# Clearing of DRAM rows moved to SyncE's queue, gelu steps moved back, the first expert's begin reordered, and the last block's second rows added by TensorE

## The reference

```python
def forward(x, ...):
    for l in range(2):
        h = rmsnorm(x, norm_mix[l])
        u = h @ w_in[l]                                   # all head groups' inputs
        a = rg_lru(causal_conv(x_lru)) * gelu(y_lru)      # recurrence, gated
        b = mla_group(q_dn, kv_dn, k_pe)                  # 6 heads, causal
        c = nsa_group(q, kc, vc, ks, vs, kw, vw, gates)   # 6 heads, three branches
        x = x + concat(a, b, c) @ w_out[l]
        h = rmsnorm(x, norm_ffn[l])
        if l == 0:
            x = x + (silu(h @ wg) * (h @ wu)) @ wd        # d_ff 2816
        else:
            top_val, top_idx = top_k(h @ router_w, 2)
            w = softmax(top_val)
            for e in range(8):                            # d_ff 1408 each
                x = x + gate[:, e] * ((silu(h @ wg[e]) * (h @ wu[e])) @ wd[e])
    return rmsnorm(x, norm_final)
```

## Time and profile before

| | us |
|---|---|
| median of 3 runs | 1330.28 |
| lowest, highest | 1328.93, 1330.73 |
| the profiled execution, its own time | 1324.21 |
| its span, first to last instruction | 1322.4 |
| TensorE busy in it | 1267.1 (96%) |
| VectorE | 949.1 (72%) |
| ScalarE | 677.8 (51%) |
| GpSimd | 130.1 (10%) |

### The profile page before, as it was taken

How to read it: one execution, slowest core, us unless ns; L and a number is a source line. 1 busy time by engine, 2 the same in 40 slices (tenths; PEclk the granted TensorE clock), 3 DMA queues, 4 the chain that set the end, 5 groups by cost and what they waited for, 6 DMA issues and landing times.

```text
span 1322.4 us, 24758 instructions
## 1 busy us (share of the span) xinstructions
PE 1267.1 (96%) x10314; PEld 819.6 (62%) x10375; DVE 949.1 (72%) x1304; ACT 677.8 (51%) x993; POOL 130.1 (10%) x113
## 2 busy tenths in 40 slices
PE   7999999999999999999999999979999999999992
PEld 3457565444444444444457565569979988989981
DVE  7886885886531556334886885688788799989996
ACT  6256774443210333112265774365586687787772
POOL 0011320600000000031011000501200000000002
PEclk9999899999999999999999999999999999999997
DMA  8551881444310443012551000168999999999975
GB/s 272 184 151 35 317 334 60 146 186 149 118 67 0 150 165 148 0 33 103 194 150 35 20 1 21 61 238 325 360 381 376 349 348 398 374 352 398 359 307 208
DMA packets 43134, 260.26 MB, mean 197 GB/s; under 512 B 6522, under 2 KB 7546, under 8 KB 28554
## 3 DMA queue, kind: packets, MB, share of 16 engines
q1 hardware_dynamic: 33626, 224.77, 46.1%
q0 software_dynamic: 8960, 33.26, 7.0%
q10 hardware_dynamic: 432, 0.59, 0.1%
HBM read 218.00 MB, written 33.65 MB: 190 GB/s over the span
## 4 chain that ended last, share of the span: by engine, by line
PE 84%; issue 6%; DVE 4%; DMA 3%; POOL 1%; ACT 1%; SPq 0%; POOLq 0%; DVEq 0%; ACTq 0%
PE bank L1177 20%; PE bank L1178 20%; PE bank L1179 19%; PE bank L1387 5%; PE bank L1435 3%; PE bank L1405 3%; PE bank L727 1%; PE bank L726 1%; PE bank L725 1%; DMA expert_slots<-arena,row_index 1%; PE bank L735 1%; PE bank L737 1%; PE bank L736 1%; POOL expert_slots L2520 1%; PE bank L1242 1%
## 5 line engine op out<-in xcount | busy, mean ns | idle before, releaser
L988 DVE SCALAR_TENSOR_TENSOR arena<-arena 128x3072 f16<-128x3072 f32 x86 | 288.2, 3352 | 10.8 <-ACT arena L842 9.1
L842 ACT ACTIVATE arena<-arena 128x3072 f16<-128x3072 f32 x86 | 237.9, 2767 | 41.1 <-DMA arena<-in_ew 19.5
L1177 PE MATMUL bank<-arena 128*128 128x144 bf16 (+3 forms) x877 | 215.1, 264 | 6.0 <-DVE arena L988 2.7
L1178 PE MATMUL bank<-arena 128*128 128x144 f16 (+3 forms) x878 | 215.4, 264 | 0.1
L1179 PE MATMUL bank<-arena 128*128 128x144 bf16 (+3 forms) x867 | 211.2, 263 | 0.0
L1178 PE MATMUL bank<-hl,wring_hi 128*128 128x512 f16 x352 | 133.4, 379 | 1.5 <-issue 0.6
L1179 PE MATMUL bank<-hh,wring_lo 128*128 128x512 bf16 x341 | 129.2, 379 | 0.0
L1177 PE MATMUL bank<-hh,arena 128*128 128x512 bf16 x338 | 128.1, 379 | 1.0
L1178 PE MATMUL bank<-hl,arena 128*128 128x512 f16 x338 | 128.1, 379 | 0.0
L1177 PE MATMUL bank<-hh,wring_hi 128*128 128x512 bf16 (+1 forms) x333 | 126.3, 379 | 1.0 <-DVE wring_lo L1885 0.5
L1179 PE MATMUL bank<-hh,arena 128*128 128x512 bf16 x319 | 120.9, 379 | 0.0
(11 more groups left out here) (334 smaller groups left out, 2521.2 us busy)
## 6 DMA issues: line engine op xcount, KB each, us to landing
arena<-in_ew SPq DMA_DIRECT2D x86, 1536.0 KB, 9.1
arena<-in_dw SPq DMA_DIRECT2D x22, 1536.0 KB, 6.4
wstage<-in_w_chunk SPq DMA_DIRECT2D x44, 512.0 KB, 3.9
expert_results<-iota POOLq DMA_DIRECT2D x9, 2048.0 KB
arena<-in_cmp_w SPq DMA_DIRECT2D x2, 2048.0 KB, 8.0
arena<-arena SPq DMA_DIRECT2D x60, 64.0 KB, 2.1
expert_slots<-iota POOLq DMA_DIRECT2D x5, 512.0 KB
expert_results<-wstage SPq DMA_DIRECT2D x5, 512.0 KB
```

The costliest lines, as they stand in the source:

```text
L842: act.activation(ew_hi_[:, G % EP, :], ew[:, G % ES, :], ACT.Copy, scale=SW).then_inc(M["hi_ready"], 1)
L988: dve.scalar_tensor_tensor(out=ew_lo_[:, G % EP, :], in0=ew[:, G % ES, :], scalar=SW, in1=ew_hi_[:, G % EP, :], op0=ALU.mult, op1=ALU.subt ...
L1177: pe.matmul(out, w_hi, x_hi, start=first, stop=False)
L1178: pe.matmul(out, w_hi, x_lo, start=False, stop=False)
```

## The change

It has five parts.

1. The 19 DMAs that clear DRAM rows are issued by SyncE (`clear_rows`) in layer 0, ahead of its load of chunk 18; GpSimd issues none. `blank` counts them alone, and `load_rows` waits for `slotted`.
2. In both layers GpSimd's gelu steps wait for the maximum of score step 3.
3. The first expert's begin: TensorE does all 64 gather products in a row and then `upper(0)` and `upper(1)`; ScalarE turns the third weight part after all eight copies, and runs a silu of one column ahead of the first part, which loads the table.
4. `places` is a generator of four parts, of which VectorE runs one in each of the steps G = 4 to 7; the row numbers come in the third, the flag in the fourth.
5. In the tail block 3 (`SUMMED`) is added by TensorE: identity times the sum with the first rows, then a diagonal matrix of the second gates times the second rows, both in fp32 into two PSUM banks, which ScalarE's square and VectorE's last scaling read. VectorE does block 3's first addition ahead of the others, makes the diagonal, and leaves out its second addition.

```diff
@@ experts_pe
             def begin():
+                pe.wait_ge(M["gathered"], KC // 2)
+                pe.wait_ge(M["first_hi"], 1)
+                upper(0)
                 pe.wait_ge(M["first_hi"], 2)
                 upper(1)
...
                 if j == KC // 2:
-                    pe.wait_ge(M["gathered"], KC // 2)
-                    pe.wait_ge(M["first_hi"], 1)
-                    upper(0)
                     pe.wait_ge(*ready("tok_l", TT - 1))
@@ experts_act
+            act.activation(small[:, 244:245], eps[:, 0:1], ACT.Silu)
             first_hi(0)
             for j in range(KC):
                 gathered(0, j, bank[GATHER_BANK[j % 4]], 0, CAPS[0])
-                if j in (3, 5):
-                    first_hi(j // 2)
-            for p in (3, 4):
+                if j == 3:
+                    first_hi(1)
+            for p in (2, 3, 4):
                 first_hi(p)
@@ experts_dve
-                if G == 2 * LEAD:
-                    places()
+                if G >= 2 * LEAD:
+                    next(place_parts, None)
@@ experts_sp, load_rows
-                sp.wait_ge(*ready("blank", "slotted"))
+                sp.wait_ge(*ready("slotted"))
@@ tensor, behind the experts
+            for i in SUMMED:
+                pe.wait_ge(*ready("first_added", i))
+                for half in range(2):
+                    pe.matmul(banks[:, 2 * i + half, :], ident[:, :], xtok[i][:, half * 4:(half + 1) * 4, :],
+                              start=True, stop=False)
+            for i in SUMMED:
+                pe.wait_ge(*ready("first_added", "diagonal", i))
+                pe.wait_ge(*ready(f"second_row{i}"))
+                for half in range(2):
+                    mm = pe.matmul(banks[:, 2 * i + half, :], diagonal[i - SUMMED[0]],
+                                   second_row[i][:, half * T:(half + 1) * T], start=False, stop=True)
+                mm.then_inc(*signal("second_summed", i))
@@ scalar, tail
-                act.wait_ge(*ready("second_added", i))
-                act.activation(xtok[i], by_chunk(second_row[i]), ACT.Square,
+                act.wait_ge(*(ready("second_summed", i) if i in SUMMED else ready("second_added", i)))
+                act.activation(xtok[i], by_chunk(with_second(i)), ACT.Square,
@@ vector, tail
-            for i in range(TT):
+            for i in (*SUMMED, *range(SUMMED[0])):
...
+            for i in SUMMED:
+                dve.tensor_scalar(diagonal[i - SUMMED[0]], ident[:, :], gate_second[:, i:i + 1], None,
+                                  ALU.mult).then_inc(*signal("first_added", "diagonal", i))
             for i in range(TT + 1):
-                if i < TT:
+                if i < SUMMED[0]:
                     dve.wait_ge(*ready(f"second_row{i}"))
@@ gpsimd, gelu steps, both layers
+                    pool.wait_ge(*ready("nmx", l, 3, 0))
                     pool.wait_ge(*ready("feat", l, feat_index("y", c)))
...
-                if l == 0:
-                    pool.wait_ge(*ready("nmx", l, 0, 0))
-                    blank = results_dram.rearrange("(p a) d -> p (a d)", p=P).rearrange("p (a n) -> p a n", n=256)
...
@@ sync
+            def clear_rows():
+                sp.wait_ge(*ready("by_pool", "zeros"))
+                blank = results_dram.rearrange("(p a) d -> p (a d)", p=P).rearrange("p (a n) -> p a n", n=256)
+                for a in range(0, blank.shape[1], 16):
+                    n = min(16, blank.shape[1] - a)
+                    sp.dma_start(blank[:, a:a + n, :], iota[:, 0:256].unsqueeze(1).broadcast_to([P, n, 256])
+                                 ).then_inc(*signal("blank", by=16))
+                for e in range(2, NE):
+                    rows = slots_dram[e * YROWS:e * YROWS + CAPS[e], :].rearrange("r (a n) -> r a n", n=256)
+                    for a in range(0, CAPS[e], P):
+                        w = min(CAPS[e] - a, P)
+                        sp.dma_start(rows[a:a + w], iota[0:w, 0:256].unsqueeze(1)
+                                     .broadcast_to([w, DM // 256, 256])).then_inc(*signal("blank", by=16))
...
+                    if l == 0 and j == NF + WR + 1:
+                        clear_rows()
```

24 lines of the change are left out of this document (11 added, 13 removed).

## The result

| | before | after |
|---|---|---|
| median, us | 1329.61 (4 runs) | 1338.70 (4 runs) |
| lowest, highest | 1328.48, 1330.73 | 1338.15, 1339.57 |
| ratio after / before | | 1.0076, 95% interval 1.0059 to 1.0092 |
| the profiled execution, its span | 1324.21, 1322.4 | 1338.5, 1336.7 |
| granted clock, mean | 0.989 | 0.976 |

The change makes the kernel 9.1 us slower; 1323.8 us with a range from 1318.5 to 1330.5 was forecast. The two profiled spans differ by more, 14.3 us, since the profiled execution of the kernel before was 5.4 us faster than its median, and that of the changed kernel was at its median.

The account below looks back on a forecast made before the run. TensorE, busy for 96% of the span, was taken as the bound, with gains only where it waits or crawls. 2.9 + 0 + 3.2 + 0.4 = 6.5 us off the median 1330.28 gave 1323.8 us, range 1318.5 to 1330.5.

Parts of the forecast that it names:

- Layer 0, clearing: Layer 0's attention: clearing DMAs issued by SyncE instead of GpSimd gain 2.9 us, bounds 0 and 2.9.
- rival 2: Layer 0 keeps its 2.9 us, since the same bytes cross the same DMA engines: 1326.7 us; 12%.
- rival 3: Chunk 18 lands late behind the clearing, and TensorE's output projection stands some 20 us: 1343 us; 4%.
- Gelu steps: Both layers' attention: later gelu steps free VectorE for 1.1 us but bring new holds; gain 0, bounds 1 us per layer.
- Rival 4: Moved gelu steps hold VectorE more than they free, 1 us or more per layer, with low clock: 1327.4 us; 9%.
- The begin: First expert's start: reordered gather products and an earlier Silu table load gain 2.0 us, between 1.3 and 2.3.
- The places: Middle of the first expert: cutting the places into four parts removes TensorE's stall, 2.4 us gained.
- The scatter: Ends at 947.5, so begin, places and scatter together gain 3.2 us; bounds 4.4 gained, 6.7 lost.
- The two floors: Estimates of the scatter's end: 946.6 from issuing the eight indirect DMAs, 946.4 from bytes at 424 GB/s.
- rival 1: Scatter ends up to 6.7 us later and the stage behind has no slack: 1333.7 us at full price; 15%.
- The tail: Behind the last expert: one VectorE addition less, two fp32 products on TensorE; 0.4 us gained, bounds +1.1 to -0.5.
- The sum: Whole kernel: 2.9 + 0 + 3.2 + 0.4 = 6.5 us gained, giving 1323.8 us.

Follow-up runs that it names:

- b_clear: The kernel before with only the 19 clearing DMAs moved to SyncE, ahead of chunk 18: 1325.47 us, 0.9977 of before.
- a_gelu: The changed kernel with GpSimd's gelu steps no longer waiting for the fourth score step's maximum: 1326.28 us, 0.9984 of before.
- a_quarter: The changed kernel with the gelu steps on 128 of 512 columns only: 2941.11 us, with later experts running overflow rounds; comparable only up to the experts.
- a_gelu6: The changed kernel with the gelu steps waiting for the seventh score step's maximum in place of the fourth's: 1324.32 us, 0.9967 of before.
- b_gelu: The kernel before with only the gelu steps made to wait for the fourth score step's maximum: 1339.48 us, 1.0075 of before.
- a_places: The changed kernel with the places worked out in one block at G = 4 again: 1335.49 us, 1.0051 of before.
- a_rows: The changed kernel with the four parts of the places reordered, row numbers in the first: 1335.62 us, 1.0038 of before.
- a_tail: The changed kernel with the old tail, VectorE adding the second rows of all four blocks: 1337.50 us, 1.0065 of before.
- best: The changed kernel without the gelu steps' wait, with row numbers in the first of four parts and the old tail: 1319.84 us, 0.9935 of before.
- a_begin: The changed kernel with the first expert's begin as before: 1338.65 us, 1.0071 of before.

## Why the prediction was wrong

- **Layer 0, clearing: right.** 2.9 us forecast; b_clear measured 2.91, a_gelu 2.92. It was the issue on GpSimd that cost, and rival 2 falls. The clearing began at 128.1, 8 us earlier than the forecast took it. Chunk 18 was never near (rival 3): the clearing moved 385 GB/s, was through before 200, and ScalarE turned the chunk at 232.37 behind TensorE.
- **Gelu steps: the step that failed.** The forecast named the mechanism, counted the hold that goes (1.1 us), set the four new ones against it and took 0, with 1 us per layer as bounds "from the 1.1 us of the one hold seen". The runs showed 5.6 us per layer. Two things were not priced: which instruction TensorE waits for next, and the clock behind its waits. The hold that goes was worth one wait of 0.68 us, which is still there in a_gelu and gone in a_quarter. The new ones make TensorE wait 0.77 and 1.59 us where layer 1 before had 0.68 and 0.22; behind that came 10.2 us at half clock in each layer, worth 5 us of TensorE's work. Rows 4 had shown that price already, in layer 0's attention. Rival 4 was this case; it had 9%, and 1.6 us for the clock in both layers together. The page "SBUF — State Buffer" of the Trainium skill, section "SBUF: two separate sides", says that GpSimd and those of VectorE's instructions that read two inputs from SBUF, or run in a mode that takes two ports, exclude each other for a whole instruction. The trace agrees: the small product is held to the end of a 1.03 us step, and maxima from PSUM are not held. That was reason not to net one hold against four.
- **The begin: 2.0 forecast, about 1.5 measured,** within its bounds. First silu and upper half came as foreseen in a_gelu, at 878.79 + 2.86 = 881.65 us; 881.6 was said.
- **The places: right.** 2.4 forecast, 2.7 measured. No wait of TensorE is left there.
- **The scatter: mis-sized.** Row numbers came when forecast (925.4; a_gelu 922.97 + 2.86 = 925.8). The two floors gave 22 us from there to the end, and 25.2 to 25.7 were measured, between them and the 32.3 of the upper bound. The eight issues took 17.3 us, as the forecast had them (17.7); the term that was too small is the end of the transfer, 3 to 4 us taken, 7.8 (a_gelu) and 8.3 measured. So in a_gelu SyncE's wait ended 0.3 us later than today (shift taken off) and not 3.2 earlier, and 2.3 later in the changed kernel, whose begin had low clock. Then the stage had no slack, as rival 1 said, and the clock fell for another 6.8 us: 5.5 us lost from s12 to s16. From w1 to s16 the changed kernel lost 2.8 us where 3.2 were to be gained; some 1.5 us of that are low clock at the begin, which the profiled execution of before happened not to have.
- **The tail: wrong in sign by the traces,** by 1 us; the medians can't tell. Block 3's rows landed 5.5 to 6.4 us after their gather's issue in seven executions, not 4.7, and the products took 3.75 us at the low clock, where the forecast had 2.3 at full and 4.5 at low clock: 0.4 us gained became 0.6 lost.
- **The sum.** From the marks: -2.9 + 2 x 5.6 - 1.5 - 2.7 + 5.5 + 0.6 = 10.2 us, beside 9.1 measured (7.8 to 12.2 by the ratio's interval). That the sum comes so near is in part luck, since one execution stands behind each mark and the begin alone moved by 1.5 us between executions. The forecast had -6.5. Rivals 1 and 4 came true together; I had priced them one at a time, as if the likeliest case excluded them, and so 8% stood for slower.

What stays open: why the low clock at the begin is missing in two of fourteen profiled executions; why it is missing behind the scatter in a_gelu6, whose waits there are longer in sum than the changed kernel's; and why a scatter that starts later ends sooner after its start. The 1.15 us by which the changed kernel is late at m3 arise ahead of every edit and are of the same kind (3.4 us of low clock from 110 on); b_gelu, a_places, a_rows and a_tail have it too, best and a_begin don't. But b_clear and a_gelu6 are 1.0 us late at m3 without it, so not all of that spread is the clock.

## What to carry to other kernels

A step on an engine that excludes another one is placed by the slack of the engine it holds: put it where the held instruction isn't the next that TensorE needs, and price every short wait of TensorE with the low clock that can follow it: here 1.5 us more of waiting became 5.6 us. When work is cut into parts to fit into gaps, put first the part for which another engine or queue waits: with the row numbers in the first of four parts the same cut gains 2.7 us and loses at most 0.8 in the stage behind. Read a second execution before taking a stretch of low clock, or its absence, for the kernel's own.

## What the runs showed of the hardware

- A GpSimd elementwise step holds VectorE's scalings, products of two SBUF operands and the weights' remainder until it ends; reciprocals (0.15) and reductions from PSUM (1.27) run through. With a quarter of the columns the product beside it takes 0.39 us in place of 1.03.
- It goes the other way too: in a_gelu6 GpSimd's scalar step takes 1.47 us in place of 0.61 while VectorE makes the weights' remainder.
- GpSimd's issues of plain DMAs hold VectorE as well: four scalings of 2.48 us in place of 1.14 before the change, a pair of 2.71 in place of 1.99 in b_gelu. The same 19 DMAs from SyncE hold nothing, though their 385 GB/s cross the same stretch.
- Eight indirect DMAs that scatter 4.2 MB take 31.9 to 32.8 us from first issue to the end of SyncE's wait when begun in the fifth step, and 25.2 to 25.7 when begun two steps later in the same stream of weight loads.
- A pair of fp32 products of 512 columns that takes 1.98 us at full clock (a_places, the identity pair of the tail) takes 3.75 at the low one.
